# High and low input of the sample's residual products side by side in one 512-column product

## The reference

```python
x = x + (mixer(rms_norm(x)) @ w_out)             # layer 0: S5 and GLA heads, layer 1: differential attention
x = x + cross_attention(rms_norm(x), rms_norm(mem), ...)      # 4 heads, 256 memory tokens, then @ w_o
x = x + jnp.square(jax.nn.relu(rms_norm(x) @ mlp_w1)) @ mlp_w2    # 1024 -> 4096 -> 1024
```

## Time and profile before

| | |
|---|---|
| time, median of 3 runs | 2402.44 us (2402.33 to 2404.04) |
| the profiled execution | 2402.41 us, of it 2400.6 us from the first to the last instruction (its span) |
| PE busy | 2389.2 us, 14327 products |
| PEld busy | 2050.2 us |
| DVE busy | 1512.3 us, 2554 instructions |
| ACT busy | 1166.6 us, 2070 instructions |

### The profile page before, as it was taken

How to read it: one execution, slowest core, us unless ns; L and a number is a source line. 1 busy time by engine, 2 the same in 40 slices (tenths; PEclk the granted TensorE clock), 3 DMA queues, 4 the chain that set the end, 5 groups by cost and what they waited for, 6 DMA issues and landing times.

```text
span 2400.6 us, 35749 instructions
## 1 busy us (share of the span) xinstructions
PE 2389.2 (100%) x14327; PEld 2050.2 (85%) x14327; DVE 1512.3 (63%) x2554; ACT 1166.6 (49%) x2070; POOL 0.2 (0%) x4
## 2 busy tenths in 40 slices
PE   9999999999999999999999999999999999999999
PEld 6988877888889998998789888888888898888887
DVE  8999668776566555664655438848985565533332
ACT  5334455555445555545454436636764453523432
POOL 0000000000000000000000000000000000000000
PEclk9999999999999999999999999999999999999999
DMA  5446533553124654443234323233234323433332
GB/s 201 106 98 164 209 110 103 165 202 123 62 88 150 192 185 132 132 133 105 76 112 149 96 88 123 89 101 100 89 100 148 122 80 117 126 98 98 97 97 89
DMA packets 109700, 291.36 MB, mean 121 GB/s; under 512 B 18944, under 2 KB 40576, under 8 KB 108256
## 3 DMA queue, kind: packets, MB, share of 16 engines
q1 hardware_dynamic: 100832, 264.83, 35.5%
q10 hardware_dynamic: 8704, 24.25, 3.3%
HBM read 267.45 MB, written 19.50 MB: 120 GB/s over the span
## 4 chain that ended last, share of the span: by engine, by line
PE 86%; DVE 3%; ACT 1%; issue 0%; DVEq 0%; ACTq 0%
PE ps L1499 74%; PE ps L1613 2%; PE ps L1570 2%; PE ps L1595 2%; PE ps L1637 1%; PE ps L1626 1%; DVE wlo L1476 1%; PE ps L1583 0%; DVE ringP L1886 0%; PE ps L1644 0%; PE ps L1991 0%; PE ps L2056 0%; PE ps L1513 0%; DVE in_lP L1893 0%; PE ps L1525 0%
## 5 line engine op out<-in xcount | busy, mean ns | idle before, releaser
L1471 ACT ACTIVATE whi<-wraw 128x1024 fp32r<-128x1024 f32 x430 | 452.1, 1052 | 183.5 <-PE ps L1499 127.1
L1499 PE MATMUL ps<-in_hP,whi 128*128 128x512 f32 x1336 | 532.8, 399 | 1.7 <-DVE in_lP L1893 0.9
L1476 DVE TENSOR_TENSOR wlo<-wraw,whi 128x1024 fp32r<-128x1024 f32 x430 | 522.9, 1218 | 3.1 <-ACT whi L1471 2.9
L1499 PE MATMUL ps<-in_hP,wlo 128*128 128x512 f32 x1336 | 520.8, 390 | 0.0
L1499 PE MATMUL ps<-in_lP,whi 128*128 128x512 f32 x1336 | 520.2, 389 | 0.0
L1499 PE MATMUL ps<-in_hS,whi 128*128 128x256 f32 x1088 | 316.0, 290 | 0.5 <-DVE x L1830 0.5
L1499 PE MATMUL ps<-in_hS,wlo 128*128 128x256 f32 x1088 | 307.7, 283 | 0.0
L1499 PE MATMUL ps<-in_lS,whi 128*128 128x256 f32 x1088 | 307.7, 283 | 0.0
L1499 PEld LDWEIGHTS ps<-in_hP,whi 128*128 128x128 f32 x1336 | 250.8, 188 | 60.5 <-issue 6.6
L1499 PEld LDWEIGHTS ps<-in_hP,wlo 128*128 128x128 f32 x1336 | 250.7, 188 | 53.5
L1499 PEld LDWEIGHTS ps<-in_lP,whi 128*128 128x128 f32 x1336 | 251.0, 188 | 51.7 <-issue 1.4
(11 more groups left out here) (494 smaller groups left out, 3662.6 us busy)
## 6 DMA issues: line engine op xcount, KB each, us to landing
wraw<-wt SPq DMA_DIRECT2D x432, 512.0 KB, 3.5
wraw<-wt ACTq DMA_DIRECT2D x17, 512.0 KB, 4.4
k_scratch<-region_P SPq DMA_DIRECT2D x16, 256.0 KB, 3.1
v_scratch<-vtmp SPq DMA_DIRECT2D x32, 128.0 KB, 3.5
x<-x_in SPq DMA_DIRECT2D x4, 768.0 KB, 7.0
x<-x_in SPq DMA_DIRECT2D x2, 1536.0 KB, 7.1
mix_mem<-mem_in ACTq DMA_DIRECT2D x1, 2048.0 KB, 15.7
region_S<-k_scratch ACTq DMA_DIRECT2D x2, 1024.0 KB, 7.1
```

Source lines behind the costliest of these rows:

```text
L1471: nc.scalar.activation(whi[:, (n + 3) % NHI, :, :], wraw[:, ws(n), :, :], ACT.Copy).then_inc(wh.sem, 1)
L1476: nc.vector.tensor_tensor(wlo[:, ws(n), :, :], wraw[:, ws(n), :, :], whi[:, (n + 3) % NHI, :, :].bitcast(F32), ALU.subtract).then_inc(wr.s ...
L1499: last = nc.tensor.matmul(ps[:, m % 2, 0:N[prod.g]], w_[:, k, :], x_[:, k, :], start=(k == 0 and j == 0), stop=(k == KT - 1 and j == 2))
```

## The change

For the sample's res products named in `WIDE`, that is all but o1 (eleven products, 88 tiles), the high and the low input are laid side by side: hid gets one tensor with the high and low part of each block next to each other, the sample's input one tensor with all high blocks ahead of all low ones. PE then multiplies the high weight with both at once, 512 columns, into the whole bank, and the low weight with the high input, 256 columns, into its first half: 16 products a tile. DVE adds the second half of the bank to x, and behind it, chained by a semaphore, the first half as before. The first add is new.

```diff
-                hid_h[g] = sb(f"hid_h{g}", [P, KT, N[g]], F32R, on=over)
-                hid_l[g] = sb(f"hid_l{g}", [P, KT, N[g]], F32R, on=over)
+                hid = sb(f"hid_{g}", [P, KT, 2, N[g]], F32R, on=over)
+                hid_h[g], hid_l[g], hid_w[g] = hid[:, :, 0, :], hid[:, :, 1, :], hid[:, :, :, :]
...
-            in_h = {"P": in_hP, "S": sb("in_hS", [P, KT, TS], F32R, on=fl)}
-            in_l = {"P": in_lP, "S": sb("in_lS", [P, KT, TS], F32R, on=fl)}
+            in_S = sb("in_S", [P, 2, KT, TS], F32R, on=fl)
+            in_h = {"P": in_hP, "S": in_S[:, 0, :, :]}
+            in_l = {"P": in_lP, "S": in_S[:, 1, :, :]}
...
+            WIDE = {WT[n] for n in ("dn00", "dn01", "dn02", "dn03", "dout", "o0", "eo", "dn10", "dn11", "dn12", "dn13", )}
...
+                    self.wide = None
+                    if g == "S" and kind == "res" and w0 in WIDE:
+                        self.wide = hid_w[g] if rhs is not None else in_S[:, :, :, :].rearrange("p z k t -> p k z t")
...
+                if prod.g == "S" and prod.wide is not None:
+                    for k in range(KT):
+                        if i == 0 and prod.ready is not None:
+                            pe.wait_ge(*prod.ready(k))
+                        nc.tensor.matmul(ps[:, m % 2, :].rearrange("p (z t) -> p z t", z=2), w_h[:, k, :], prod.wide[:, k, :, :],
+                                         start=(k == 0), stop=False)
+                        last = nc.tensor.matmul(ps[:, m % 2, 0:N["S"]], w_l[:, k, :], h_[:, k, :], start=False, stop=(k == KT - 1))
+                    last.then_inc(td.sem, 1)
+                    return
...
+                    if g == "S" and prod.wide is not None:
+                        dve_chain(nc.vector.tensor_tensor(x[:, i, cols(g)], ps[:, b, TS:2 * TS], x[:, i, cols(g)], ALU.add))
                     nc.vector.tensor_tensor(x[:, i, cols(g)], ps[:, b, 0:N[g]], x[:, i, cols(g)], ALU.add).then_inc(tf[b].sem, 1)
```

More of the change, by code:

```diff
@@ L975, in trunk_tail @@
             fl = ExitStack()
-            hid_h, hid_l, R = {}, {}, {}
+            hid_h, hid_l, hid_w, R = {}, {}, {}, {}
             for g, words in (("P", 12288), ("S", 6144)):
                 over = ExitStack()
-                hid_h[g] = sb(f"hid_h{g}", [P, KT, N[g]], F32R, on=over)
-                hid_l[g] = sb(f"hid_l{g}", [P, KT, N[g]], F32R, on=over)
+                hid = sb(f"hid_{g}", [P, KT, 2, N[g]], F32R, on=over)
+                hid_h[g], hid_l[g], hid_w[g] = hid[:, :, 0, :], hid[:, :, 1, :], hid[:, :, :, :]
                 over.close()
```

## The result

The changed kernel takes 2409.11 us (median, 2407.50 to 2411.39), the kernel before 2402.51 us beside it: a ratio of 1.0027 with an interval of 1.0018 to 1.0035, or 6.5 us slower (4.3 to 8.4). The profiled execution has a span of 2407.6 us against 2400.6. The predicted time was 2403.3 us, and its range ended at 2408.5.

What follows compares the result with a forecast made beforehand. PE was taken as the bound. PE-bound products -4.3, down product 3 +1.5, down product 2 +2.5, mixer output +2.0, diff output 0, down products 0 and 1 -0.8: +0.9 us on 2402.4 gives 2403.3 us, range 2398.5 to 2408.5.

Steps and rivals of the forecast that it cites:

- PE's part: In the eleven products, one 512- and one 256-column product replace three of 256: 0.360 to 0.347 us, 0.107 us a tile.
- the five PE-bound products: Layer-0 down products and first cross output: PE's gain comes through in all 40 tiles, -4.3 us.
- dn10 and dn11: Down products 0 and 1 of layer 1, under the prompt's diff attention: two of four tiles gain, -0.8 us.
- dout: Diff output: delay from the added adds behind a late weight tile is cancelled two tiles later, 0 us.
- eo: Mixer output: DVE adds without a gap, so six added adds delay the prompt's product, +2.0 us.
- dn12: Down product 2 of layer 1: six added adds on DVE's gapless stretch delay the query product, +2.5 us.
- dn13: Down product 3 of layer 1: five added adds delay the prompt's second up tile, +1.5 us.
- PE-bound stretches hide the second add: Layer-0 down products and first cross output: DVE has 0.46 us a tile to spare, so the add costs nothing.
- All of PE's gain: Rival, all eleven products: the whole 9.4 us comes through, 2393.0 us; chance 9%.
- The wide product saves nothing: Rival, wide products: each half pays the fixed cost, 0.240 us a product, 2408.4 us; chance 6%.
- Slower under the diff attention: Rival, down products 0 and 1 of layer 1: added adds delay each next maximum, 7.3 us more, 2411.4 us; chance 7%.

Runs made afterwards that it cites:

- the flat run: The changed kernel, with the eight down products' wide input and output given as one run of 512 columns: 2408.63 us against 2403.87, ratio 1.0021.
- the best kernel: Changed kernel with eight products wide, widths grouped except in each product's first tile, key and value loads behind the diff output: 2399.68 us against 2402.96, ratio 0.9982.

## Why the prediction was wrong, point by point

**PE's part, "0.227 + 0.120 = 0.347": mis-sized by half where it counts.** Both numbers are right, each for a run of its own width. The step added them as if a product's price did not depend on the one ahead of it, and did not say so; a row that bore on it stood in the trace of before, at 2049.11. The sum itself, 0.347, is the price of the 19 fast tiles, but all of the layer-0 down products, dn10 and dn11 ran at 0.353. So the five PE-bound products gained 2.3 us instead of 4.3, and dn10 and dn11 together 0.33 instead of 0.8. Grouped the tile takes 2.79 us, near the predicted 2.77. The Trainium skill, "TensorE: Matmul & The Clock Gate", section "Wait — 56ns, not 53.3ns?", gives a fixed cost of about 2.5 ns for a product. By an estimate from that figure a tile would gain 8 x 2.5 ns = 0.02 us. The trace does not agree: a tile gained 0.053 us or 0.107 alternating, and 0.087 grouped.

**dout, "0 us, between -0.9 and +0.4": wrong, +3.2.** The step took the low part's start at 1265.76 as fixed and asked only what 0.46 us of second add do behind it. That part came out exactly: 1267.08 to 1269.10 is 2.02 us, against 1.56 in before. But the start itself moved, by 1.32 us. The bound had "if the weights land earlier" on its one side and no later landing on the other, though the rows showed a transfer that was late already, with the loads of keys and values under way beside it. Without the wait the tile of 1269.25 would have started 2.00 us earlier, at 1267.25, which is 0.40 before its 1267.65. Sum of the delay: 1.32 (later low part) + 0.46 (second add) + 0.40 (PE is earlier there) - 0.18 (what PE came later than that add allowed in before: 1267.65 against 1267.32 + 0.15) = 2.00 us, as measured. The weight tile came 1.32 us later although its load was issued 0.20 us earlier (1256.13 against 1256.33): it was 9.84 us on its way instead of 8.32. In both it lands 0.2 us behind the second load of keys and values, and without these loads it takes 3.4 us. That it collides with them is shown; what sets how long is not. The loads were issued 0.31 us later in after, but with dout alone they stand to the tile as in after, 1.74 us ahead of it against 1.75, and it took 8.76 us. Over the kernels with a wide dout and the loads ahead of it, it is 8.76 to 10.29 us. The clock behind the wait, some 1.5 us, was in no term.

**eo, dn12, dn13: right.** Predicted +2.0, +2.5 and +1.5; measured +2.07, +2.43 and, with the prompt's first tiles, +1.40 + 0.34. The price of a second add, 0.46 us chained, shows in after as 0.45 from start to start. The reading behind them, that DVE is full in these three stretches whatever its average says, is borne out by the run without the second add, where all three come out below before.

**PE-bound stretches hide the second add: right.** The run without it has the same o0, dn00 to dn03, dn10 and dn11, to 0.05 us.

**The rivals.** All of PE's gain: no. The wide product saves nothing, 2408.4 us: its time is near the measured one, but by chance; the product does save, half, and the rest of the loss is dout's. Slower under the diff attention: no, dn10 and dn11 gain 0.17 us each.

With the measured price of a pair and dout's term left at 0, the prediction's own sum is -2.3 + 1.5 + 2.5 + 2.0 - 0.3 = +3.4 us. The run with the late loads is after without dout's collision, and its span is 2404.1, 3.5 us above before; by the medians it is 1.9 us (ratio 1.0009, 0.0 to 4.6 us). There dout gains 0.43 us, which the sum has at 0. So within about 0.5 us by the stretches the sum lacks nothing but the one collision.

## What to carry to other kernels

The price of a product read from a run of like products holds for such a run; where a change makes widths alternate, look for a change of width in the trace and give the price a range, since here one alternation had two prices. Keeping like widths together gave the four layer-0 down products 0.24 us each once the first tile was left alternating. A transfer that is late but covered is not a fixed time: bound it on both sides, and price what waits behind it in the order of the engine that it holds up. An extra instruction on a part-busy engine costs nothing where its stretch has gaps and its full length where it has none, so use it by stretch: five to eight of the eleven products were worth the change.

## What the hardware showed unexpectedly

**The same alternation of 512 and 256 columns ran at two prices.** A pair takes 0.353 us in most tiles and 0.347 in the others; a wide product then keeps PE for 0.236 or 0.230 us, in a long run of its own width for 0.227, and a narrow one for 0.117 instead of 0.120. In before, the five 512-column products behind a change of width take 0.232 on average. The form of access is not the cause (the flat run has both prices too); what in PE is, was not tried.

**The granted clock fell to 1.2 GHz behind the longest waits of PE in dout, not behind the shorter ones.** After waits of 1.84 us (after) and 2.43 us (all products grouped) it fell, after 0.76, 1.34 and, in dn12, 1.40 us it did not. Five cases are no rule. It also fell without any wait in stretches that no kernel here changes; windows of the kernel with five wide products and of the best kernel, in the same place:

```profile
408.50:415.30 6.80, 6.80 (x16) 4.97 (x16) 4.84 (x8) 3.52 (x5) 0.00 (x0) 0.52 0.00 0
```

```profile
406.00:416.00 10.00, 10.00 (x50) 7.09 (x49) 6.44 (x8) 5.90 (x9) 0.00 (x0) 1.00 0.06 9
```

The first profile is 3.2 us longer by that alone, those without the second add and with dout alone 1.65. Differences of this size between two profiles are therefore read stretch by stretch here, and not from the spans.
